# Output product and router of a hybrid layer joined in one program, by token tile, and a reordered start of the experts

## What is computed

```python
att = rmsnorm(att, attn_norm_w)                       # 512 x 512
rk = (group_norm(y) * ln_w + ln_b + bonus) * (sigmoid(dg) @ g2)   # 512 x 512
h = x + concatenate([att, rk], axis=-1) @ w_o         # 1024 x 1024 weights
hn = rmsnorm(h, norm2_w)
logits = hn @ router_w + router_b                     # top 4 of 32, softmax
h = h + moe(hn, ...)                                  # up 1024 -> 2048, clamped SwiGLU, down 1024 -> 1024
out = rmsnorm(h, final_norm_w)
```

## Time and profile before

| | |
|---|---|
| median of 3 runs | 1864.51 us (1862.79 to 1867.49) |
| the profiled execution's own time | 1864.29 us |
| its span | 1862.1 us |
| of that outside the span | 2.19 us |
| PE / DVE / ACT busy | 90% / 81% / 60% |

### The profile page before, as it was taken

One profiled execution on the slowest core, in us unless ns is written; L12 is line 12 of the kernel. 1 busy time (PEld: TensorE's weight loads), 2 busy tenths in 40 slices (PEclk: granted clock), 3 DMA queues, 4 the chain that ended last, 5 costly groups with the idle time before them and its releaser, 6 DMA issues. The chain is left out here.

```text
span 1862.1 us, 34230 instructions
## 1 busy us (share of the span) xinstructions
PE 1673.8 (90%) x12595; PEld 1357.3 (73%) x12596; DVE 1501.7 (81%) x1713; ACT 1118.5 (60%) x1096; POOL 284.6 (15%) x188
## 2 busy tenths in 40 slices
PE   5997788888939579999999999999999999999992
PEld 4886566767728448888888888888888888888881
DVE  4554787786572459999999999999999999999992
ACT  4343543343331247777777777777777777777772
POOL 0000352351200021111112111111111211211100
PEclk9999798999959669999999999999999999999996
DMA  5331000000040869999999999999999999999993
GB/s 158 94 100 52 8 28 11 20 19 8 15 153 1 286 182 340 382 380 370 378 374 379 366 384 378 368 382 378 360 381 378 370 368 377 380 363 380 381 329 103
DMA packets 207518, 473.06 MB, mean 254 GB/s; under 512 B 18646, under 2 KB 29348, under 8 KB 207244
## 3 DMA queue, kind: packets, MB, share of 16 engines
q1 hardware_dynamic: 197068, 442.51, 64.8%
q0 software_dynamic: 9792, 27.28, 6.6%
q10 hardware_dynamic: 576, 2.10, 0.3%
HBM read 454.12 MB, written 26.08 MB: 258 GB/s over the span
## 5 line engine op out<-in xcount | busy, mean ns | idle before, releaser
L1826 DVE TENSOR_TENSOR moe_w_lo<-w_raw,moe_w_hi 128x2048 fp32r<-128x2048 f32 x384 | 867.8, 2287 | 54.0 <-ACT moe_w_hi L1822 52.2
L1822 ACT ACTIVATE moe_w_hi<-w_raw 128x2048 fp32r<-128x2048 f32 x384 | 735.6, 1916 | 126.5 <-PE bank L1843 122.5
L1840 PE MATMUL bank<-moe_w_hi,moe_x_hi 128*128 128x512 f32 x1024 | 406.2, 397 | 0.0
L1843 PE MATMUL bank<-moe_w_lo,moe_x_hi 128*128 128x512 f32 x1024 | 400.4, 391 | 0.0
L1841 PE MATMUL bank<-moe_w_hi,moe_x_lo 128*128 128x512 f32 x1024 | 399.9, 391 | 0.0
L1843 PEld LDWEIGHTS bank<-moe_w_lo,moe_x_hi 128*128 128x128 f32 x1024 | 192.9, 188 | 41.2
L1841 PEld LDWEIGHTS bank<-moe_w_hi,moe_x_lo 128*128 128x128 f32 x1024 | 193.2, 189 | 38.5
L1840 PEld LDWEIGHTS bank<-moe_w_hi,moe_x_hi 128*128 128x128 f32 x1024 | 193.0, 189 | 38.4
L1905 POOL DMA_INDIRECT moe_x_gathered<-hn_rows,moe_gather_rows x32 | 71.7, 2241 | 908.7 <-DVE moe_gather_rows L1893 907.7
L1840 PE MATMUL bank<-moe_w_hi,moe_a_hi 128*128 128x512 f32 x512 | 209.0, 408 | 1.4 <-DVE moe_a_lo L1877 1.4
L1843 PE MATMUL bank<-moe_w_lo,moe_a_hi 128*128 128x512 f32 x512 | 200.7, 392 | 0.0
(11 more groups left out here) (326 smaller groups left out, 2255.4 us busy)
## 6 DMA issues: line engine op xcount, KB each, us to landing
w_raw<-in_expert_w_up SPq DMA_DIRECT2D x512, 512.0 KB, 8.7
w_raw<-in_expert_w_down SPq DMA_DIRECT2D x256, 512.0 KB
proj_w_raw<-in_w_in SPq DMA_DIRECT2D x36, 384.0 KB, 3.3
mixer_bias_table<-in_att_bias SPq DMA_DIRECT2D x16, 256.0 KB, 2.7
mix_wo_raw<-in_w_o SPq DMA_DIRECT2D x8, 512.0 KB, 8.1
x<-in_x ACTq DMA_DIRECT2D x4, 512.0 KB, 4.5
x<-in_x SPq DMA_DIRECT2D x1, 2048.0 KB
sum_rows<-x SPq DMA_DIRECT2D x1, 2048.0 KB, 15.1
```

Source lines behind the costliest of these rows:

```text
L1822: act.activation(w_hi[:, j % RING, :], raw[:, j % RAW, :], ACT.Copy).then_inc(hi_w[j % RING], 1)
L1826: eng.tensor_tensor(w_lo[:, j % RING, :], raw[:, j % RAW, :], w_hi[:, j % RING, :].bitcast(F32), ALU.subtract)\
L1840: pe.matmul(out, s_hi[:, k, :], w_hi[:, j % RING, w], start=first, stop=False)
L1843: ins = pe.matmul(out, s_hi[:, k, :], w_lo[:, j % RING, w], start=False, stop=ends)
```

## The change

`mixed_output` and `router` become one program, `mix_router`. The operands of the mixer (`PTb`, `att`, `rk`, the scan's reset row) now lie in the memory of `w_raw`, so that all 8 blocks of split W_o fit; raw W_o goes through `x`, and x is loaded again after it, tile by tile. The product runs tile by tile, with the attention half of the next tiles between the RWKV halves. h is turned without its norm: `norm2_w` is multiplied into the router's weights, and the root is applied to the logits. In `experts` the own-bias product of tile 3 moves behind three weight slots, the overflow table moves behind the last block, the bias tables are loaded here, only four slots are loaded ahead, POOL no longer waits for the last scatter (SP does), and the empty loop has 15 // 5 = 3 turns. The sigmoid of the gate moves to the mixer's start.

```diff
+    for k in range(4):
+        use(("c", k), 2 + k)
+    use(("g", 0), 6)
+    for t in range(3):
+        for n in range(2):
+            use(("o", t, n), 2 * t + n)
+    for t in range(NT):
+        use(("rk", t), 7)
+        if t + 1 < NT:
+            use(("g", t + 1), 6)
+    for n in range(2):
+        use(("o", 3, n), n)
+    for t in range(NT):
+        for h in range(2):
+            use(("x", t, h), (4 if t == 2 else 2) + h)
+        use(("l", t), 6 + t % 2)
...
+        @block.sync
+            load_wo(0)
+            load_wo(1)
+            sp.dma_start(g2[:, :], ext["g2"]).then_inc(g2_in, 16)
+            load_wo(2)
+            load_wo(3)
...
+            for k in range(NS, KD):
+                load_wo(k)
+            for t in range(NT):
+                sp.wait_ge(lo_w[NS + t], 1)
+                sp.dma_start(x[:, t, :], xd[:, t, :]).then_inc(x_in[t], 16)
...
+            store_rows(0)
+            store_rows(1)
+            key = ("rk", NT - 1)
+            sp.wait_ge(B.free_sem(key), B.after(0, key))
+            first_weights(0, 1, 2)
+            store_rows(2)
+            first_weights(3)
+            store_rows(3)
...
+        @block.gpsimd
+                pool.tensor_tensor(h3(VN[:, t, :]), h3(VN[:, t, :]),
+                                   coef[:, t, :].unsqueeze(2).to_broadcast([P, NH, HD]), ALU.mult).then_inc(bon, 1)
...
+        @block.tensor
+            gate(0)
+            part(0, (0, 1, 2, 3))
+            part(1, (0, 1))
+            turn_rk(0)
+            gate(1)
+            part(1, (2, 3))
+            part(0, (4, 5, 6, 7))
+            part(2, (0, 1))
+            turn_rk(1)
+            gate(2)
+            part(2, (2, 3))
+            part(1, (4, 5, 6, 7))
+            part(3, (0, 1))
+            turn_rk(2)
+            gate(3)
+            part(3, (2, 3))
+            part(2, (4, 5))
+            turn_rk(3)
+            turn_h(0)
+            part(2, (6, 7))
+            logits(0)
+            part(3, (4, 5))
+            turn_h(1)
+            part(3, (6, 7))
+            logits(1)
+            turn_h(2)
+            logits(2)
+            turn_h(3)
+            logits(3)
...
+        @block.vector
+            centre(0)
+            centre(1)
+            dve.wait_ge(asum, NT)
+            dve.tensor_scalar(ss[:, :], ss[:, :], 1.0 / C, RMS_EPS, ALU.mult, ALU.add).then_inc(avar, 1)
+            dve.wait_ge(aroot, 1)
+            ch(dve.reciprocal(ss[:, :], ss[:, :]))
+            for t in range(NT):
+                dve.tensor_scalar(att[:, t, :], att[:, t, :], ss[:, t:t + 1], None, ALU.mult).then_inc(an, 1)
+            split_w(0)
+            centre(2)
+            split_w(1)
+            att_lo(0)
+            att_lo(1)
+            split_w(2)
+            att_lo(2)
+            split_w(3)
+            att_lo(3)
+            variance(0)
+            variance(1)
+            centre(3)
+            variance(2)
+            variance(3)
+            finish_rk(0)
+            for k in range(4, KD):
+                split_w(k)
+            rk_lo(0)
+            finish_rk(1)
+            rk_lo(1)
+            finish_rk(2)
+            add_h(0)
...
+            h_norm(0)
+            add_h(1)
+            rk_lo(2)
+            finish_rk(3)
+            h_norm(1)
+            rk_lo(3)
...
+            add_h(2)
+            choose(0)
+            h_norm(2)
+            add_h(3)
+            choose(1)
+            h_norm(3)
+            choose(2)
+            choose(3)
...
-            pool.wait_ge(scattered, 16 * n + 16)
-            pool.sem_inc(rows_out, 1)
+            if not last:
+                pool.wait_ge(scattered, 16 * n + 16)
+                pool.sem_inc(rows_out, 1)
...
             for j in range(4):
+                if j == 3:
+                    own_bias(NT - 1)
                 slot_matmuls(pe, 0, j, pro, 0, keys, x_hi, x_lo, 2 * j)
...
             split_hi(act, 0, 0)
+            split_hi(act, 0, 1)
             own_bias(0)
+            split_hi(act, 0, 2)
             own_bias(1)
-            split_hi(act, 0, 1)
+            split_hi(act, 0, 3)
             own_bias(2)
-            own_bias(3)
-            split_hi(act, 0, 2)
             for i in range(2):
                 take_hi(act, pro, 0, (0, f"X{i}"), x_hi, i, hi_x)
-            for j in range(3, 7):
+            split_hi(act, 0, 4)
+            own_bias(3)
+            for j in range(5, 7):
                 split_hi(act, 0, j)
...
-            for j in range(3):
+            for j in range(4):
                 split_lo(dve, 0, j)
-            overflow(dve)
             for i in range(2):
                 take_lo(dve, pro, 0, (0, f"X{i}"), x_hi, x_lo, i, hi_x, i + 1)
-            split_lo(dve, 0, 3)
...
+            if what == "dve":
+                overflow(eng)
             eng.wait_ge(ovd, 2)
...
             sp.wait_ge(fw_in, 16)
+            sp.wait_ge(scattered, 16 * E)
+            sp.sem_inc(rows_out, 1)
             sp.wait_ge(ovd, 2)
```

More of the change, by code:

```diff
@@ L1648, in _, with bank @@
-            pe.wait_ge(c_in, 16 * 6)
-            for k in range(KD):
-                pe.wait_ge(B.free_sem(("t", k)), B.after(0, ("t", k)))
-            for t in range(NT):
-                key = ("l", t)
-                for k in range(KD):
-                    ins = pe.matmul(B.tile(key)[:, 0:E], hT[:, k, P * t:P * t + P], rw[:, k, :], start=(k == 0), stop=(k == KD - 1))
-                ins.then_inc(B.fill_sem(key), 1)
+            def bank(key):
+                pe.wait_ge(B.free_sem(key), B.before(0, key))
+                return B.tile(key)
@@ new lines, in logits @@
+            def logits(t):
+                key = ("l", t)
+                dst = bank(key)
+                if t == 0:
+                    pe.wait_ge(rwd, 1)
+                for k in range(KD):
+                    if k % 4 == 0:
+                        half = ("x", t, k // 4)
+                        pe.wait_ge(B.free_sem(half), B.after(0, half))
+                    ins = pe.matmul(dst[:, 0:E], hT[:, t % 2, k, :], rw[:, k, :], start=(k == 0), stop=(k == KD - 1))
+                ins.then_inc(B.fill_sem(key), 1)
@@ L2041, in pool_block @@
                 pool_gather(pool, B, it, (par, "M"))
-            pool_scatter(pool, n, B, it, par)
+            pool_scatter(pool, n, B, it, par, B is main and not nxt)
         def first_pe(pe):
@@ L2231, in _ @@
                 pool.sem_inc(used[r], 1)
-            for r in range(RAW):
+            for r in range(NFIRST):
                 pool.sem_inc(raw_in[r], 32)
@@ new lines, in build @@
+        keep["spare"] = shared[:, at:at + T]
+        keep["VN"] = keep["PTb"][:, TRV - TR:TRV - TR + 4, :]
+        with ExitStack() as first:
+            keep["PTa"] = sb("proj_att", [P, N_ATT_TILES, T], c=first)
+            in_projection(nc, psum, ext, keep, bias_dram)
+            mixer(nc, psum, ext, keep)
+        for name, shape, dt in (("posm", [P, NT, E], F32), ("meta", [P, NT, E, 5], BF16), ("iota", [P, T + P], F32),
+                                ("lim", [P, 1 + NT], F32), ("own_rows", [P, NT], I32), ("dense", [P, NT, E], F32),
+                                ("counts", [P, E], F32), ("order", [P, NOV], F32)):
+            keep[name] = sb(name, shape, dt)
```

611 lines of the change are left out of this document (321 added, 290 removed).

## The result

The changed kernel takes 1808.93 us (median of 4 runs, 1807.52 to 1811.81) against 1864.94 for the kernel before, a ratio of 0.9701 (95% interval 0.9683 to 0.9719). The forecast was 1810.0. Its profiled execution took 1809.95 us.

A forecast was written before the change was run, and what follows sets the result against it. Expert loop bound by PE and left alone; gains before and after it: 39.3 + 9.2 + 6.0 - 0.3 = 54.2 us, so a span of 1807.9 and, with 2.2 around it, 1810; range about 1801 to 1832.

The forecast's parts named there:

- Rival D: Expert loop becomes bound by transfers, at SP's slot loads with four slots in hand; 1875 us at 2.1 more a block; chance 0.02.
- The stage: Output stage and router joined, from 519.8: experts' start forecast at 613.4, 39.3 us earlier than 652.7.
- rivals A: Small turns and waits in the joined stage keep PE's clock down, 192 matmuls cost 38 us more: 1850; chance 0.10.
- C: DVE and PE wait for each other at each turn in the joined stage: 1840 us; chance 0.07.
- DVE's first list: DVE's splits, centrings, rests and first tile's finish in the joined stage: about 23.3 us from 527.5, so 550.8.
- PE's list: From 550.8 PE leads the joined stage with 144 matmuls, turns, gates and logits: 41.7 us, product ends at 592.5.
- The contention: At the joined stage's start, POOL's bonus multiplies hold two centring subtractions on DVE: 2.2 us, two times 1.07.
- The waits in PE's list: In the joined stage, PE waits 1.5 us for the first tile and 1.0 us at its RWKV half.
- The start: Experts' start: first slot product at 17.8 us, 11.3 earlier; moved own-bias tile between slots costs 2.1; net 9.2.
- Rival B: Experts' start and end give nothing: gather queues behind 3 MB of weights (+9), drain hangs on landing (+4.7): 1824; chance 0.15.
- The end: After the last scatter, POOL skips its wait, fewer empty turns, drain of equal length to 1839.3: 6.0 us earlier.
- Before the stage: Gate's sigmoid moved to the mixer's start costs up to one ACT pass: 0.3 us.

## Why the prediction was right

**What bounds it.** The claim was that the loop stays as it is and that all of the gain lies ahead of it and behind. PE is busy 1123.37 of 1125 us in the loop. A block takes 35.65 us (gathers at 719.99 and 1718.22, 28 blocks apart) against 35.70, which makes the 1.30 of the table; it wasn't forecast and has no explanation here. Rival D, transfers, is off: DMA share 1.03, and no wait.

**The stage.** 93.6 us forecast from the stage's start to the experts, 90.94 measured, 91.2 on the average; rivals A (half clock throughout) and C (lists that lock) are off. DVE's first list: first rest 31.0 forecast, done at 553.4 - 523.0 = 30.4. PE's list from there to the last product: 41.7 forecast, 594.1 - 553.4 = 40.7 measured. The tail to the last logits: 12.0 forecast, 605.1 - 594.1 = 11.0 measured, since the clock fell only ahead of the last tile and not behind the last product. Against before, the saving depends on the execution that it is measured from: 132.85 us there in the first trace, 129.36 in the second. Of these 38 to 42 us the runs took back only the alternation, 7.0; that the rest comes from PE's product running over DVE's work and from the passes that fell away is read from the rows, and no run splits it further.

**The contention** was a term of 2.2 us, from a row of the mixer. The runs give 1.9 on DVE and 1.7 on the stage; each subtraction was held 0.80 us and not 1.07, and small steps beside them made up the rest. The Trainium skill ("SBUF — State Buffer", Who interferes with whom) has it that a two-input pass of DVE contends with a GpSimd read and a reduction does not; the rows agree, with 1.49 against 0.69 for the one and 0.67 to 0.69 for the other. One thing goes beyond what I took from it: the small step between them, with one input, took 0.95 and 0.30 in place of 0.17.

**The waits in PE's list.** Forecast 1.5 us at the first turn and 1.0 at the first rest, measured 4.0 and 0. The sum was nearly the same, so the stage came out right, but the split mattered to whoever wants to do better: it was the 4.0 that could be filled. The 6 us of DVE at `rk_lo(1)` were 6.44.

**The start** is the step that failed by its size: 9.2 us forecast, 7.15 measured in the first trace and 7.7 between the averages. Its first part was right (first slot product at 17.8 forecast, 17.62 measured; 11.3 earlier forecast, 11.5 measured). What failed was "2.1" as the whole cost of the tile between the slots. The tile itself cost 1.9 to 2.0. What was left out is the copy on ACT that waits for the tile, and the splits queued behind the copy: 1.8 us more, shown by moving the copy alone. I had costed the moved instruction on its own engine only. Rival B, the gather behind 3 MB of weights, is off: PE waits 0.22 us for it.

**The end**: 6.0 us saved by forecast, 7.06 measured. The prediction gives two figures that don't agree: 6.0 less than the 17.08 of before is 11.1 from the issue to the next phase, and its list of signs says 10, which by its own path (1839.3 - 1829.4 = 9.9) is the end of the drain, with the next phase 1.2 us behind as before. So the 10.02 measured hits the sign by luck. The path that I wrote down has POOL in its drain 4.3 us after the issue, for 5.62 us; on the chip POOL gets there 2.4 us sooner (it goes on at 1782.0, as the scatter is issued, where I had 1.6 us behind, and a turn takes 0.45 us and not 0.63) and stays 1.3 longer, so the drain ends 1.1 sooner. Rival B had the drain hang on the landing and give back 4.7 us. Its end does keep step with the landing, but 2.8 us behind it, and 7.06 were saved all the same.

**Before the stage**: 0.3 us for the sigmoid. The first traces differ by ten times that, and the repeated runs showed that their difference means nothing.

## What to carry to other kernels

When a step is moved to another place in the lists, follow every engine that takes part in it. The matmuls that were moved here cost 1.9 us on PE, and the copy on ACT that takes their result cost 1.8 more, because it stood ahead of splits which didn't need it; a consumer goes behind all that is ready without it. Where an engine waits and its list holds ready work behind the wait, move that work ahead: 12 matmuls moved gave 3.6 us, more than the wait itself got shorter. And before a small difference between two traces is explained, run both kernels again and cut the spans at marks: here one and the same code reached the same mark 6 us apart.

## What the runs showed that I had not expected

- POOL's drain at the end of a phase in which it issued a scatter: 5.62 us where the scatter had landed long before, 6.9 to 8.0 where POOL came within 2 us of the issue, with an end 8.8 to 9.2 us after it, 2.7 to 2.8 us behind the landing each time.
- The part ahead of the changed stage ends between 519.8 and 529.5 us over all executions, with the granted clock in one 40 us stretch of the mixer at 0.76 in one of them and 0.99 in another.
- An empty turn of the overflow loop takes POOL 0.63 us in the kernel before and 0.45 to 0.48 in the changed one.
